# A fused two-block transformer kernel: the moving weights of the 512-column split products are read in another order

## The chip, the cores and the metric

The kernel runs on one core of one Trainium2 chip. The metric is the device time of one execution in microseconds. A core has TensorE (matrix products: it loads a 128 x 128 stationary operand and streams the columns of a moving operand past it), VectorE, ScalarE, GpSimd and a queue engine (SP) from which most DMAs are issued. Products write to PSUM, which VectorE and ScalarE read.

## The reference

One sequence of 256 tokens of width 2048 goes through two blocks in fp32. What matters here are the large projections and what is done with them:

```python
x = x + mix @ w_out[i]                                            # 2048 x 2048
h2 = rms_norm(x, mlp_norm[i])
x = x + jnp.square(jax.nn.relu(h2 @ w_ffn_up[i])) @ w_ffn_down[i]  # 2048 x 8192 x 2048
gate = jax.nn.sigmoid(rms_norm(x, ple_norm[i]) @ w_ple_gate[i])
x = x + gate * (p[i] @ w_ple_proj[i])
...
h = x + jnp.concatenate([gla_out, nsa_out], axis=-1) @ w_out
m = rms_norm_2(h, ffn_norm_g)
return h + (jax.nn.silu(m @ w_gate) * (m @ w_up)) @ w_down         # 2048 x 5632 x 2048
```

Between them stand the mixers (a causal pool, a chunked recurrence, gated linear attention, compressed and windowed attention).

## The kernel before, in words

Every engine has one program, written out by hand, and the programs meet at semaphores. Weights come through a ring of two slots in SBUF, each 16 tiles of 128 x 512, in groups numbered `n`. A slot has four units of 2,048 elements per partition. Each large product is a split one: the fp32 operand is held as a rounded part (`wh`, type fp32r) and the rest (`wl`), and `three` (L621) issues three fp32r products, high x high, high x low and low x high, into one sum in PSUM. ScalarE makes the high part of a unit (`high`, L1366), VectorE subtracts it to get the low part (`low`, L1899), in place in the ring; TensorE waits for `w_low`, uses the unit and reports `w_used`, upon which the next weights are loaded.

There are two kinds of split product. In `split_rows` (L628) the weights are stationary and 256 tokens move: FFN up projections, gates and inputs. In `split_tokens` (L665), and in two loops written like it for the second output projection (`first_half`, L1222, and the loop at L1307), the tokens are stationary and 512 columns of weights move: the output projections, the down projections of both FFNs and the PLE gate. The sums of these lie in two PSUM banks, one per half of the tokens (`pair[0]` and `pair[1]` in turn, `first_sums` in the attention stage), 512 neighbouring columns each. All products of both kinds are issued from L625.

VectorE adds the finished sums to the residual `xs` in chunks of 512 columns (`add_out`, L1901, and `add_first`, L2459), and in the PLE gate ScalarE takes them through a sigmoid into `gate_sb` (L1620). A pair of banks is written again after the addition of the call before last (`sum_step`). In the gate stage plain fp32 products with 512 columns (`project`, L1005, issued at L1012) stand among the split ones.

Of the kernel before, what the change touches and what calls it, by code (L numbers as in the profile page):

```python
# [14 lines left out]
ALU = mybir.AluOpType  # L15
ACT = mybir.ActivationFunctionType
# [6 lines left out]
KT = D // P  # L23
# [98 lines left out]
def build(nc, inp, consts, out):  # L122
# [26 lines left out]
    xs = sbuf("xs", [P, TT, D])  # L149
    actT = sbuf("actT", [P, KT, T], (0, KT * T))  # L150
# [47 lines left out]
    def along(ap, n):  # L198

        return ap.unsqueeze(len(ap.shape)).broadcast_to(list(ap.shape) + [n])  # L200

    ident, tri, eye64 = con("ident"), con("tri"), con("eye64")
    pair = [PS[:, 0:2, :], PS[:, 2:4, :]]
# [110 lines left out]
    rs_fin, rs_n4, rs_sq, rs_gate, rs_n5, scaled_ss = (small[:, 88 + 2 * i:90 + 2 * i] for i in range(6))  # L314
# [61 lines left out]
    gate_sb = split(actf[:, 3072:4096], (TT, CW))  # L376
# [34 lines left out]
    first_sums = [PS[:, 4:6, :], PS[:, 6:8, :], PS[:, 4:6, :], PS[:, 4:6, :]]  # L411

    XD, HD = area(XH_AT + 16, KT, T), area(0, KT, T)
    XH2 = HD
# [188 lines left out]
    def _(pe):  # L603
# [17 lines left out]
        def three(dst, weights, tokens, first, last, early=False):  # L621

            (wh, wl), (xh, xl) = weights, tokens
            for q, (w, x) in enumerate(((wh, xh), (wh, xl), (wl, xh))):
                mm = pe.matmul(dst, r32(w, early), r32(x, early), start=first and q == 0, stop=last and q == 2)  # L625
            return mm
# [38 lines left out]
        def split_tokens(n, out, xh, xl, i=None, per=2, units=UNITS[4], ready=None, after=None):  # L665

            for q, j in enumerate(units):
                pe.wait_ge(S["w_low"], split_count(n, j, i, per))
                if ready is not None:
                    ready(q)  # L670
                wh, wl = (a.rearrange("p (k n) -> p k n", k=4) for a in (high_home(n, i, j), unit_at(n % 2, j)))
                for k in range(4):
                    for t in range(TT):
                        x, tok = 4 * q + k, slice(t * P, (t + 1) * P)
                        mm = three(out[:, t, :], (xh(x)[:, tok], xl(x)[:, tok]), (wh[:, k, :], wl[:, k, :]),
                                   x == 0, x == 4 * len(units) - 1)
                mm.then_inc(S["w_used"], counts(units, j))
                if after and q in after:
                    after[q]()
# [42 lines left out]
        for t in range(2):  # L722
            mm = pe.transpose(PS[:, 5, t * P:(t + 1) * P], prow[:, t, :], ident)
# [46 lines left out]
        for g in range(2 * (NCH - 1)):  # L770
            c, m0 = g // 2, g % 2 * 4
            if g >= 4:
                pe.wait_ge(S["bk_copied"], g - 3)
            for m in range(4):
                mm = pe.transpose(PS[:, 4 + g % 4, m * P:(m + 1) * P], BK[:, m0 + m, c, :], ident)
# [123 lines left out]
        for c in range(NCH):  # L899
# [4 lines left out]
            for m in range(HM):  # L904
                for e in range(2):
                    mm = pe.matmul(PS[HALF[e], 0, m * C:(m + 1) * C], G[:, m, e, c, 0:C], UV(c)[:, m, e, :],
                                   start=True, stop=True)
# [7 lines left out]
            for m in range(HM):  # L915
                for e in range(2):
                    mm = pe.matmul(PS[HALF[e], 1, m * C:(m + 1) * C], DTi[HALF[e], m, c, :], ZSB[HALF[e], m, :],
                                   start=True, stop=True)
# [5 lines left out]
            if c < NCH - 1:  # L924
                for m in range(HM):
                    for e in range(2):
                        mm = pe.matmul(PS[HALF[e], 2, m * C:(m + 1) * C], BKtok(c)[:, m, e * C:(e + 1) * C],
                                       UV(c)[:, m, e, :], start=True, stop=True)
# [34 lines left out]
        for t in range(TT):  # L963
            pe.wait_ge(S["gate_copied"], t + 1)
            pe.wait_ge(S["yn_ready"], t + 1)
            for m in range(HM):
                mm = pe.transpose(PS[:, 4 + 2 * t + m // 4, m % 4 * P:(m % 4 + 1) * P], Ytok[:, t, m * P:(m + 1) * P], ident)
# [82 lines left out]
        for n in range(N_KCVC, N_GOQ):  # L1050
# [3 lines left out]
            if n == N_KSVS:  # L1054
                pe.wait_ge(S["w_low"], NARROW)
                for k in range(KT):
                    mm = three(PS[0:SWM, 4, 0:T], (SWH[:, k, :], SW[:, k, :]), (XH[:, k, :], actT[:, k, :]),
                               k == 0, k == KT - 1)
# [3 lines left out]
        for h in range(GH):  # L1062
            mm = pe.matmul(PS[:, 6 + h // 2, h % 2 * T:(h % 2 + 1) * T], GW2[:, h * P:(h + 1) * P], LR, start=True, stop=True)
        mm.then_inc(S["low_rank"], 1)
        for t in range(TT):
            mm = pe.transpose(PS[:, 5, t * 24:t * 24 + 24], LRG[32:SWM, t * P:(t + 1) * P], ident[32:SWM, 32:SWM])
# [77 lines left out]
        for i in range(2):  # L1144
            mm = pe.matmul(PS[:, 4 + i, :], con("ones"), KSQ[:, 2 * i:2 * i + 2, :].rearrange("p a b -> p (a b)"),
                           start=True, stop=True)
        mm.then_inc(S["k_sums"], 1)
        pe.wait_ge(S["nsq_ready"], 2)
        for t in range(TT):
            for h in range(NH):  # L1150
                mm = pe.matmul(PS[:, 6, t * NH + h:t * NH + h + 1], QSQ[:, h, t * P:(t + 1) * P], con("ones")[:, 0:1],
                               start=True, stop=True)
# [5 lines left out]
        for t in range(TT):  # L1158
            for h in range(GH):
                mm = pe.transpose(PS[:, 6 + t, h * P:(h + 1) * P], K4[:, h, t * P:(t + 1) * P], ident)  # L1160
# [16 lines left out]
        for i in range(2):  # L1177
            mm = pe.transpose(PS[:, 2, i * CB:(i + 1) * CB], PTAB[i], ident[0:CB, 0:CB])
# [35 lines left out]
        for t in range(TT):  # L1214
            pe.wait_ge(S["on_ready"], t + 1)
            for m in range(8):
                at = m % 2 * T + t * P
                mm = pe.transpose(PS[:, 4 + m // 2, at:at + P], OT[:, t, m * P:(m + 1) * P], ident)
# [3 lines left out]
        def first_half(*qs):  # L1222

            for q in qs:
                n, j, e, c = N_OUT2 + q // 8, q % 8 // 2, q % 2, q // 4
                if q % 4 == 0 and c >= 2:
                    pe.wait_ge(S["sum_step"], SUM["first2"] + 2 * c - 3)
                pe.wait_ge(S["w_low"], half_count(n, q % 8))
                if q < 4:
                    pe.wait_ge(S["gla_low"], q + 1)  # L1230
                if q == 0:
                    pe.wait_ge(S["on_read"], 4)
                wh, wl = (a.rearrange("p (k n) -> p k n", k=2) for a in (HIO[q % 4], half_at(n % 2, q % 8)))
                for k in range(2):
                    for t in range(TT):
                        x, tok = 2 * (q % 4) + k, slice(t * P, (t + 1) * P)
                        mm = three(first_sums[c][:, t, :], (XH2[:, x, tok], actT[:, x, tok]), (wh[:, k, :], wl[:, k, :]),
                                   x == 0, x == 7)
                mm.then_inc(S["w_used" if e else "half_used"], 1)

        first_half(0)
# [65 lines left out]
        for c in range(4):  # L1307
            n = N_REST2 + c // 2
            if c >= 2:
                pe.wait_ge(S["sum_step"], SUM["out2"] + c - 1)  # L1310
            for j in (2 * (c % 2), 2 * (c % 2) + 1):
                pe.wait_ge(S["w_low"], split_count(n, j))
                wh, wl = (a.rearrange("p (k n) -> p k n", k=4) for a in (high_home(n, i, j), unit_at(n % 2, j)))
                for k in range(4):
                    for t in range(TT):
                        x, tok = 8 + j % 2 * 4 + k, slice(t * P, (t + 1) * P)
                        mm = three(pair[c % 2][:, t, :], (XH2[:, x, tok], actT[:, x, tok]), (wh[:, k, :], wl[:, k, :]),
                                   x == 8, x == KT - 1)
                mm.then_inc(S["w_used"], 1)
                if j % 2 == 0 and c:  # L1320
                    turn("n5", c - 1)
# [34 lines left out]
    def _(act):  # L1356
# [59 lines left out]
        for j in range(1, KT // 2, 2):  # L1416
            act.wait_ge(S["norm_turned"], j + 1)
            for q in range(2):
                k = 2 * j + q
# [79 lines left out]
        for g in range(2 * (NCH - 1)):  # L1499
            c, m0 = g // 2, g % 2 * 4  # L1500
# [52 lines left out]
        for c in range(NCH):  # L1553
# [13 lines left out]
            if c % 2:  # L1567
                t = c // 2
# [38 lines left out]
        for c in range(4):  # L1607
            n = N_GATE + c
            high(n, (3,))
            if c == 0:  # L1610
                norm_chunk("n3", "ple_norm", 3)
                root("n3")
            else:
                norm_chunk("n4", None, c - 1)
            high(n + 1, (0, 1, 2))
            act.wait_ge(S["w_used"], used(n))
            act.wait_ge(S["rs_ready"], 2)
            act.wait_ge(S["sum_step"], SUM["gate"] + c)
            for t in range(TT):
                ins = act.activation(gate_sb[:, t], pair[c % 2][:, t], ACT.Sigmoid, scale=rs_gate[:, t:t + 1])  # L1620
            ins.then_inc(S["groups_read"], 1)
        def high_half(n, *qs):

# [222 lines left out]
    def _(v):  # L1846
# [54 lines left out]
        def add_out(w, g, at, by=None):  # L1901


            v.wait_ge(S["w_used"], w)
            if by is None:
                ins = v.tensor_tensor(xs[:, :, at], pair[g], xs[:, :, at], ALU.add)
            else:
                for t in range(TT):
                    ins = v.scalar_tensor_tensor(xs[:, t, at], pair[g][:, t], by[:, t:t + 1], xs[:, t, at], ALU.mult, ALU.add)  # L1909
            ins.then_inc(S["sum_step"], 1)  # L1910

        def columns(c):
            return slice(CW * c, CW * (c + 1))
# [545 lines left out]
        def add_first(c):  # L2459
            v.wait_ge(S["w_used"], 4 * N_OUT2 + 2 * c + 2)  # L2460
            for t in range(TT):
                r = xs[:, t, columns(c)]
                ins = v.scalar_tensor_tensor(r, r, rs_fin[:, t:t + 1], first_sums[c][:, t], ALU.mult, ALU.add)
            ins.then_inc(S["sum_step"], 1)

        def o_norm(t):
# [297 lines left out]
```

## Time and profile before

| | |
|---|---|
| median of 3 runs | 2439.66 us (2433.91 to 2442.28) |
| the profiled execution | 2437.74 us, span 2435.6 us |
| TensorE products busy | 2395.8 us, 98% of the span, 18,076 of them |
| weight loads busy | 2194.3 us, 90% |
| VectorE, ScalarE, GpSimd busy | 1358.3, 987.4, 191.5 us |
| HBM read | 420.75 MB, 174 GB/s over the span |

A group's row of the profile names the line, the engine, the operation, what it writes and reads, the shape and the count, then the busy time and the mean duration of one. Durations of products overlap, so the distance between the starts of two is read from the timeline.

### The profile page before, as it was taken

The numbers are of one execution on the slowest core, as the hardware profiler recorded it, in microseconds if no ns is written. First come the engines' busy times: TensorE is split into PE (matmuls) and PEld (weight loads), VectorE is DVE, ScalarE is ACT, GpSimd is POOL, SyncE is SP. The second block draws the span as 40 slices with busy tenths as digits, with TensorE's granted clock in tenths as the row PEclk, the third lists the DMA queues.
The fourth block names the chain that finished last, engine by engine and source line by source line (L and its number), as shares of the span: only waits on it lengthen the run. The fifth ranks groups of instructions, "written<-read, shape, count | busy, mean of one in ns | idle before, by whom it ended". The sixth has DMA issues, their size and how long they took to land.

```text
span 2435.6 us, 39206 instructions
## 1 busy us (share of the span) xinstructions
PE 2395.8 (98%) x18076; PEld 2194.3 (90%) x18076; DVE 1358.3 (56%) x1134; ACT 987.4 (41%) x932; POOL 191.5 (8%) x139
## 2 busy tenths in 40 slices
PE   8998999999999999999999999999999999999999
PEld 7997888998998998988789999877998999999897
DVE  5597665544454444455457568575554554555553
ACT  4652244443333333344453364265433333433332
POOL 0003110020110110210000002000000000000000
PEclk9999999999999999999999999999999999999999
DMA  7553146665656656664556544244554754755644
GB/s 219 167 161 88 31 174 217 185 202 182 202 188 195 198 184 202 181 239 173 190 150 201 178 141 140 89 152 140 173 191 163 234 192 163 229 181 178 214 158 138
DMA packets 334528, 425.36 MB, mean 175 GB/s; under 512 B 4185, under 2 KB 249357, under 8 KB 333981
## 3 DMA queue, kind: packets, MB, share of 16 engines
q1 hardware_dynamic: 333053, 418.55, 53.2%
q0 software_dynamic: 1136, 4.17, 0.6%
q8 instruction: 142, 2.33, 0.4%
q10 hardware_dynamic: 176, 0.14, 0.0%
q14 instruction: 21, 0.17, 0.0%
HBM read 420.75 MB, written 2.10 MB: 174 GB/s over the span
## 4 chain that ended last, share of the span: by engine, by line
PE 90%; DVE 5%; issue 2%; ACT 2%; DMA 0%; POOLq 0%; POOL 0%; DVEq 0%; ACTq 0%
PE PS L625 81%; PE PS L824 1%; PE PS L715 1%; DVE ring_r L1941 1%; PE PS L661 1%; PE PS L1012 1%; PE PS L1292 0%; DVE ring_r L2249 0%; PE PS L1196 0%; ACT arena_r L1366 0%; DVE arena L2052 0%; PE PS L896 0%; PE PS L951 0%; PE PS L1120 0%; PE PS L943 0%
## 5 line engine op out<-in xcount | busy, mean ns | idle before, releaser
L625 PE MATMUL PS<-arena_r,arena_r 128*128 128x256 f32 (+1 forms) x6944 | 1544.2, 300 | 3.7 <-DVE ring_r L2249 1.4
L625 PEld LDWEIGHTS PS<-arena_r,arena_r 128*128 128x128 f32 x6944 | 1123.5, 188 | 60.2 <-issue 4.3
L1899 DVE TENSOR_TENSOR ring_r<-ring,arena_r 128x2048 fp32r<-128x2048 f32 x316 | 730.5, 2315 | 658.7 <-ACT arena_r L1366 658.7
L1366 ACT ACTIVATE arena_r<-ring 128x2048 fp32r<-128x2048 f32 (+1 forms) x394 | 691.6, 1761 | 977.0 <-PE PS L625 971.4
L625 PE MATMUL PS<-arena_r,ring_r 128*128 128x256 f32 x3072 | 852.3, 277 | 0.0
L625 PEld LDWEIGHTS PS<-arena_r,ring_r 128*128 128x128 f32 x3072 | 578.5, 188 | 0.0
L625 PE MATMUL PS<-ring_r,arena_r 128*128 128x512 f32 (+1 forms) x1504 | 539.0, 371 | 0.0
L625 PE MATMUL PS<-arena_r,actT_r 128*128 128x512 f32 (+1 forms) x1184 | 454.3, 384 | 0.0
L625 PEld LDWEIGHTS PS<-ring_r,arena_r 128*128 128x128 f32 x1504 | 275.8, 188 | 49.7 <-issue 1.4
L625 PEld LDWEIGHTS PS<-arena_r,actT_r 128*128 128x128 f32 x1184 | 222.3, 188 | 44.6
L625 PE MATMUL PS<-actT_r,arena_r 128*128 128x256 f32 (+1 forms) x656 | 184.5, 281 | 0.0
L625 PE MATMUL PS<-ring_r,actT_r 128*128 128x256 f32 x832 | 156.5, 290 | 6.6 <-DVE ring_r L1941 6.6
L625 PE MATMUL PS<-ring_r,ring_r 128*128 128x256 f32 x512 | 146.0, 285 | 0.0
L625 PEld LDWEIGHTS PS<-ring_r,actT_r 128*128 128x128 f32 x832 | 132.3, 196 | 9.3 <-DVE ring_r L1941 7.2
L625 PEld LDWEIGHTS PS<-actT_r,arena_r 128*128 128x128 f32 (+1 forms) x656 | 123.8, 189 | 0.0
L2249 DVE TENSOR_TENSOR ring_r<-ring,arena_r 128x1024 fp32r<-128x1024 f32 x56 | 72.6, 1313 | 60.0 <-ACT arena_r L1366 59.9
L625 PEld LDWEIGHTS PS<-ring_r,ring_r 128*128 128x128 f32 x512 | 99.3, 194 | 0.0
L1941 DVE TENSOR_TENSOR ring_r<-ring,actT_r 128x2048 fp32r<-128x2048 f32 x26 | 59.5, 2292 | 40.4 <-ACT actT_r L1366 40.2
L2692 POOL TENSOR_TENSOR arena_r<-arena 128x1024 fp32r<-128x1024 f32 x16 | 30.3, 1895 | 612.6 <-ACT arena L1605 612.6
L2733 POOL TENSOR_TENSOR arena_r<-arena,cst 128x1024 fp32r<-128x1024 f32 x9 | 23.0, 2552 | 690.0 <-DVE arena L2637 690.0
L1909 DVE SCALAR_TENSOR_TENSOR xs<-PS,small,xs 128x512 f32<-128x512 f32 x64 | 45.1, 747 | 40.1 <-PE PS L625 40.1
L1366 ACT ACTIVATE actT_r<-ring 128x2048 fp32r<-128x2048 f32 x26 | 49.8, 1920 | 42.9 <-PE PS L625 42.9
(339 smaller groups left out, 1403.6 us busy)
## 6 DMA issues: line engine op xcount, KB each, us to landing
ring<-in_w_ffn_up SPq DMA_DIRECT2D x32, 2048.0 KB, 10.3
ring<-in_w_ffn_down SPq DMA_DIRECT2D x32, 2048.0 KB, 8.1
ring<-in_w_in SPq DMA_DIRECT2D x22, 2048.0 KB, 8.3
ring<-in_w_gate SPq DMA_DIRECT2D x22, 2048.0 KB, 8.1
ring<-in_w_up SPq DMA_DIRECT2D x22, 2048.0 KB, 8.1
ring<-in_w_in SPq DMA_DIRECT2D x32, 1024.0 KB, 5.3
ring<-in_w_out SPq DMA_DIRECT2D x16, 2048.0 KB, 8.2
ring<-in_w_down SPq DMA_DIRECT2D x12, 2048.0 KB, 8.1
```

What stands on the lines that cost most here:

```text
L625: mm = pe.matmul(dst, r32(w, early), r32(x, early), start=first and q == 0, stop=last and q == 2)
L661: mm = pe.transpose(PS[:, 8 - banks + j % banks, q * T + t * P:q * T + (t + 1) * P], xs[:, t, k * P:(k + 1) * P], ident)
L715: mm = pe.matmul(half(0)[0:n, f, :], wag[:, k, f * P:f * P + n], actT[:, k, :], start=(k == 0), stop=(k == KT - 1))
L824: mm = pe.matmul(PS[h, bank, at:at + C], lhs(h, m, c, e), rhs(h, m, c, e), start=True, stop=True)
L1012: mm = pe.matmul(PS[:, 4 + t, :], pT[:, k, t * P:(t + 1) * P], pproj[:, c, k, :], start=(k == 0), stop=(k == 1))
L1366: return act.activation(dst, src, ACT.Copy, scale=scale)
L1899: v.tensor_tensor(r32(u), u, high_of(high_home(n, i, j)), ALU.subtract).then_inc(S["w_low"], counts(units, j))
L1909: ins = v.scalar_tensor_tensor(xs[:, t, at], pair[g][:, t], by[:, t:t + 1], xs[:, t, at], ALU.mult, ALU.add)
L1941: v.tensor_tensor(r32(w), w, high_of(high_at(u), True), ALU.subtract).then_inc(S["in_low"], 1)
L2249: v.tensor_tensor(r32(u), u, high_of(HIH[q % 4]), ALU.subtract).then_inc(S["w_low"], 1)
L2692: pool.tensor_tensor(r32(XD[:, 4 * c:4 * c + 4]), r, r, ALU.mult)
L2733: pool.tensor_tensor(r32(HD[:, 4 * m:4 * m + 4]), RQ[1], one, ALU.mult).then_inc(S["ffn2_high"], 1)
```

## The change

The moving weights of all products with 512 columns are read through a view: where columns 0, 1, 2, ... 511 went in that order, now 0, 128, 256, 384, 1, 129, 257, 385, ... go. So the sum of column 128 h + i lies at place 4 i + h of its PSUM bank, and all readers of these sums take them with a step of four, and write the residual or the gate in the old order. The stationary operands, the number of products, of columns and of elements, and all waits stay as they are.

```diff
+    def woven(ap):
+        return ap.rearrange("p (h i) -> p i h", h=4)
+    def unwoven(ap):
+        return ap.rearrange("p (i h) -> p h i", h=4)
+    def halves_of(ap):
+        return ap.rearrange("p (h i) -> p h i", h=4)
...
@@ split_tokens; first_half and the loop after the attention alike
-                        mm = three(out[:, t, :], (xh(x)[:, tok], xl(x)[:, tok]), (wh[:, k, :], wl[:, k, :]),
-                                   x == 0, x == 4 * len(units) - 1)
+                        mm = three(out[:, t, :], (xh(x)[:, tok], xl(x)[:, tok]),
+                                   (woven(wh[:, k, :]), woven(wl[:, k, :])), x == 0, x == 4 * len(units) - 1)
...
@@ the sigmoid of the gate, ScalarE
-                ins = act.activation(gate_sb[:, t], pair[c % 2][:, t], ACT.Sigmoid, scale=rs_gate[:, t:t + 1])
+                ins = act.activation(halves_of(gate_sb[:, t]), unwoven(pair[c % 2][:, t]), ACT.Sigmoid, scale=rs_gate[:, t:t + 1])
...
@@ add_out, VectorE; add_first alike
             if by is None:
-                ins = v.tensor_tensor(xs[:, :, at], pair[g], xs[:, :, at], ALU.add)
+                r = xs[:, :, at].rearrange("p t (h i) -> p t h i", h=4)
+                ins = v.tensor_tensor(r, pair[g].rearrange("p t (i h) -> p t h i", h=4), r, ALU.add)
             else:
                 for t in range(TT):
-                    ins = v.scalar_tensor_tensor(xs[:, t, at], pair[g][:, t], by[:, t:t + 1], xs[:, t, at], ALU.mult, ALU.add)
+                    r = halves_of(xs[:, t, at])
+                    ins = v.scalar_tensor_tensor(r, unwoven(pair[g][:, t]), by[:, t:t + 1], r, ALU.mult, ALU.add)
```

## Rows read from the trace of the kernel before

**Rows 1.** The page's parts 1 and 2: busy time, busy tenths, granted clock.
```profile
PE 2395.8 (98%) x18076; PEld 2194.3 (90%) x18076; DVE 1358.3 (56%) x1134; ACT 987.4 (41%) x932; POOL 191.5 (8%) x139
...
PEclk9999999999999999999999999999999999999999
```
**Rows 2.** The page's part 4: the chain that ended last.
```profile
PE 90%; DVE 5%; issue 2%; ACT 2%; DMA 0%; POOLq 0%; POOL 0%; DVEq 0%; ACTq 0%
PE PS L625 81%; PE PS L824 1%; PE PS L715 1%; DVE ring_r L1941 1%; PE PS L661 1%; PE PS L1012 1%; PE PS L1292 0%; DVE ring_r L2249 0%; PE PS L1196 0%; ACT arena_r L1366 0%; DVE arena L2052 0%; PE PS L896 0%; PE PS L951 0%; PE PS L1120 0%; PE PS L943 0%
```
**Rows 3.** Groups of TensorE products by form: count, busy us, mean ns, idle before.
```profile
L625 PE MATMUL PS<-arena_r,arena_r 128*128 128x512 f32 x1344 | 508.8, 393 | 1.6 <-DVE actT_r L2626 1.2 <-DVE actT_r L2541 0.5
L625 PE MATMUL PS<-ring_r,arena_r 128*128 128x512 f32 x1248 | 486.7, 390 | 0.0
L625 PE MATMUL PS<-arena_r,actT_r 128*128 128x512 f32 x1120 | 436.2, 389 | 0.0
...
L625 PE MATMUL PS<-arena_r 128*128 128x512 f32 x32 | 13.1, 408 | 0.0
```
**Rows 4.** Timeline of TensorE, a down projection's beginning and end: start, us, what.
```profile
704.58 0.39 PE L625 MATMUL PS<-arena_r,arena_r 128*128 128x256 f32 x2
...
704.92 0.39 PE L625 MATMUL PS<-arena_r,arena_r 128*128 128x512 f32 x1
...
791.97 0.39 PE L625 MATMUL PS<-arena_r,arena_r 128*128 128x256 f32 x2
```
**Rows 5.** The instructions of L625 within 704.92 to 791.96: min/median/max ns.
```profile
L625 PE MATMUL PS<-arena_r,arena_r x129: 276/389/393, 704.7 to 791.3; 128*128 128x512 f32 x128, 128*128 128x256 f32 x1
```
**Rows 6.** Timeline of the gate stage: first split product, and what follows 72.
```profile
1185.70 0.79 PE L625 MATMUL PS<-arena_r,arena_r 128*128 128x512 f32 x1
...
1202.74 0.82 PE L661 MATMUL PS<-cst,xs 128*128 128x128 f32 x6
```
**Rows 7.** Windows over down projections: busy us of PE, PEld, DVE, ACT, POOL, clock, DMA.
```profile
530.60:617.60 87.00, 87.00 (x386) 72.05 (x385) 42.05 (x23) 31.59 (x17) 5.80 (x2) 1.00 0.60 193
...
704.92:791.96 87.04, 87.04 (x386) 72.09 (x385) 42.04 (x23) 31.59 (x17) 5.80 (x2) 1.00 0.60 193
1841.05:1906.35 65.30, 65.30 (x291) 54.08 (x290) 34.09 (x20) 21.09 (x11) 3.87 (x1) 1.00 0.59 199
```
**Rows 8.** What TensorE waited for: us in total, times, longest.
```profile
PE PS L685 <- DMA arena<-in_attn_norm: 8.5, 1, 8.5
```
**Rows 9.** Timeline of weight loads around the plain fp32 products of L1012.
```profile
1167.70 0.19 PEld L1012 LDWEIGHTS PS<-arena 128*128 128x128 f32 x1 [0.24 <-issue]
...
1170.71 0.19 PEld L625 LDWEIGHTS PS<-ring_r,arena_r 128*128 128x128 f32 x1 [0.24 <-issue]
```
**Rows 10.** GpSimd's groups with 240 elements: step of 64 bytes, and neighbours.
```profile
L2725 POOL COPY arena<-arena 128x240 f32<-128x240 f32 x8 | 9.3, 1211 | 21.9 <-PE PS L1102 21.9
...
L2681 POOL TENSOR_SCALAR xs<-xs 128x240 f32<-128x240 f32 x8 | 6.5, 810 | 0.1
```
**Rows 11.** VectorE's level products, L2325: min/median/max ns.
```profile
L2325 DVE TENSOR_TENSOR arena<-arena x6: 684/684/685, 1443.0 to 1479.4; 128x512 f32<-128x512 f32 x6
```
**Rows 12.** The page's part 5: the subtraction that makes the low parts.
```profile
L1899 DVE TENSOR_TENSOR ring_r<-ring,arena_r 128x2048 fp32r<-128x2048 f32 x316 | 730.5, 2315 | 658.7 <-ACT arena_r L1366 658.7
```
**Rows 13.** The readers of the sums, by line: min/median/max ns.
```profile
L1909 DVE SCALAR_TENSOR_TENSOR xs<-PS,small,xs x64: 741/744/753, 552.6 to 2431.7; 128x512 f32<-128x512 f32 x64
...
L1906 DVE TENSOR_TENSOR xs<-PS,xs x8: 1217/1221/1226, 374.9 to 1709.0; 128x1024 f32<-128x1024 f32 x8
...
L1620 ACT ACTIVATE actT<-PS,small x8: 667/679/687, 1167.5 to 1252.8; 128x512 f32<-128x512 f32 x8
```
**Rows 14.** The chain's last pieces.
```profile
2424.83 6.13 PE PS L625 x27
...
2430.99 0.75 DVE xs L1909
2431.74 0.66 DVEq L2738
```

More of the change, by code:

```diff
@@ L1236, in first_half @@
                         x, tok = 2 * (q % 4) + k, slice(t * P, (t + 1) * P)
-                        mm = three(first_sums[c][:, t, :], (XH2[:, x, tok], actT[:, x, tok]), (wh[:, k, :], wl[:, k, :]),
-                                   x == 0, x == 7)
+                        mm = three(first_sums[c][:, t, :], (XH2[:, x, tok], actT[:, x, tok]),
+                                   (woven(wh[:, k, :]), woven(wl[:, k, :])), x == 0, x == 7)
                 mm.then_inc(S["w_used" if e else "half_used"], 1)
@@ L1316, in _ @@
                         x, tok = 8 + j % 2 * 4 + k, slice(t * P, (t + 1) * P)
-                        mm = three(pair[c % 2][:, t, :], (XH2[:, x, tok], actT[:, x, tok]), (wh[:, k, :], wl[:, k, :]),
-                                   x == 8, x == KT - 1)
+                        mm = three(pair[c % 2][:, t, :], (XH2[:, x, tok], actT[:, x, tok]),
+                                   (woven(wh[:, k, :]), woven(wl[:, k, :])), x == 8, x == KT - 1)
                 mm.then_inc(S["w_used"], 1)
@@ L2461, in add_first @@
             for t in range(TT):
-                r = xs[:, t, columns(c)]
-                ins = v.scalar_tensor_tensor(r, r, rs_fin[:, t:t + 1], first_sums[c][:, t], ALU.mult, ALU.add)
+                r = halves_of(xs[:, t, columns(c)])
+                ins = v.scalar_tensor_tensor(r, r, rs_fin[:, t:t + 1], unwoven(first_sums[c][:, t]), ALU.mult, ALU.add)
             ins.then_inc(S["sum_step"], 1)
```

## The prediction

> **What bounds the kernel now.** I read the page first. TensorE's matmul row is busy for 98% of the span, the weight loads for 90%, VectorE for 56%, ScalarE for 41%, and the granted clock stands in the top tenth in all 40 slices [rows 1]. The chain that ended last is 90% TensorE, 81% of it on L625, the one line from which all split products are issued [rows 2]. The groups by form say what that line holds: 3,744 products with 512 moving columns (the four forms of [rows 3] whose shape ends in 512, 1,344 + 1,248 + 1,120 + 32) and a larger number with 256. Counting the loops that the diff edits gives the same number: 16 calls x 96 in the first FFN, 4 x 96 in the first output projection, 4 x 96 in the gate, 12 x 72 and 4 x 48 in the second FFN, 16 half units x 12 and 8 units x 24 in the second output projection, which is 3,744. So every 512-column product is touched and no 256-column one.
>
> A duration in a group's row (389 ns) is not what a product costs, since products overlap. The cost is the distance from one start to the next. I took it from the timeline where nothing else is in the way: the down projection of the first FFN's second part begins at 704.92 and ends where the next 256-column product begins, at 791.97 [rows 4], and the query of the line in that stretch counts 128 products with 512 columns in the form of its first row [rows 5]; two further forms take turns with it, so there are 384: 87.05 / 384 = 226.7 ns. The windows show the same for the first FFN's first part (87.00 us) and for the first part of the second FFN, 288 products in 65.30 us, 226.7 ns each [rows 7]; I count three such groups of each, 3 x 384 + 3 x 288 = 2,016 products. In the gate stage 72 products take from 1185.70 to 1202.74 [rows 6], 236.7 ns each, and nobody waits there either. I put the other 1,728 products at the middle of the two, 231.7, which makes a mean of (2,016 x 226.7 + 1,728 x 231.7) / 3,744 = 229 ns, 857 us in all, a third of the span.
>
> The other engines have room in such a stretch: with 87.04 us of TensorE go 42.04 of VectorE, 31.59 of ScalarE, and a DMA share of 0.60 [rows 7]. TensorE is idle for 2435.6 - 2395.8 = 40 us of the whole run [rows 1], and its longest wait for others is 8.5 us, at the start [rows 8]. So the time of this kernel is the number of products times their distance, and the question is what the new order of reading does to that distance.
>
> **The change, part by part.**
>
> *The order in which the moving weights are read.* Nothing is added or removed: the same 3,744 products, the same 512 columns, the same weight loads. Only the address steps: now each column is 4 bytes behind the one before; after the change each is 128 elements (512 bytes) on, and every fourth one comes back to the line next to where it was. No row of this trace has a TensorE operand read like that. I bound it from both sides.
>
> The nearest row on the same engine is the plain fp32 projection in the gate stage, which reads the same 4-byte elements. Its products start 0.43 us apart: from 1167.70 to 1170.71 are seven steps, 430 ns for 512 columns, 0.84 ns a column [rows 9]. This is one column for each period of the lower level of 1.2 GHz, while the granted clock is at 2.4 GHz, so it is the data type's pace. Half of it, one column a period of 2.4 GHz, would be 215 ns. The split products ask for one 4-byte column in 0.42 ns and get one in 0.443 (226.7 / 512): 6% short, and 10% short in the gate stage, where the operands lie in other places and nothing else differs. Both say that these products already run at the limit of the path that brings their operands from SBUF, and that this path minds addresses. A path that is short by 6% when neighbours are read in turn has nothing in hand for a worse order. If each column then needs an access of its own and gets one per period of 1.2 GHz, a product takes the 430 ns of the plain one. Cost: 3,744 x (430 - 229) = +753 us.
>
> The other rows on strides are of other engines. GpSimd copies 240 elements that lie 64 bytes apart in 1,211 ns, and scales 240 neighbours in 810 [rows 10]: 1.5 times. On TensorE that factor would be 343 ns a product (1.5 x 229), 3,744 x 114 = +427 us. VectorE pays nothing for a small step: the level products go down to single elements two apart, and all six forms stay at 684 to 685 ns for 512 elements [rows 11]. But VectorE takes an element in no less than 1.1 ns (2,048 in 2,315 ns [rows 12]), less than half TensorE's demand, so its rows can't excuse TensorE. The lower end is a gain: if the lost 6% comes from reading neighbours in turn, the new order may give it back, down to 215 ns, 3,744 x (215 - 229) = -52 us. The upper end is the 430 ns with the same 6% on top, 453 ns, 3,744 x 224 = +839 us. Of 215, 229, 343, 430 and 453 I take 430, because it is a pace that this engine shows for this element size and because the two 4-byte reads in one period of 1.2 GHz that the present pace needs are what neighbours in one line can give and elements 512 bytes apart cannot.
>
> The Trainium skill ("Advanced Engine Details and Errata", SBUF Cachelines) states that SBUF has lines of 16 bytes, and that a reader needs at least two hits on a line to absorb the access latency. The new order hits each line once before it leaves it. No row here shows that on TensorE. By that rule the sum has the sign that I give it; it names no factor.
>
> *Taking the sums out of PSUM with a step of four.* The additions to the residual (64 of 744 ns on L1909, 8 of 1,221 on L1906, and 8 on L2463 like those of L1909) and the sigmoid (8 of 679 on L1620) read PSUM 16 bytes apart now [rows 13]. Their element counts stay. No row reads PSUM so; bounds are nothing (VectorE's step of two was free) and twice the streaming part, some 0.5 us for 512 elements. What hides it: sums alternate between two pairs of banks, and a pair is wanted again only a whole call later, 21.8 us (96 x 226.7), while VectorE is idle for half of the stretch [rows 7]. Without that cover it would be 64 x 0.5 = 32 us. Only the last two additions are in the open: the chain ends with 6.13 us of products, 0.75 of L1909 and the store [rows 14]. That is 0 to +1 us; I take 0.
>
> *What follows elsewhere.* With slower products ScalarE, VectorE and the DMAs only gain slack. In the attention stage, whose 192 products stand between other waits, longer fillers can cover at most a part of TensorE's 40 idle us; I take off 0.
>
> **The sum.** The profiled execution took 2437.7 us (span 2435.6), 2 us under the median of 2439.7. 2437.7 + 753 = 3190 us.
>
> **Rivals.**
>
> *The order gives the lost share back (faster).* For it: the 6% is lost only where columns are read at 0.44 ns, never in the plain rows, whose 430 is exactly two periods a column, so it is a matter of how the elements come, and the gate stage proves that addresses change it. Against it: nothing shows that jumping is better than walking. It would take the product to 215 ns: 2437.7 - 52 = 2386 us. It decides as soon as a product comes out under 226 ns. The Trainium skill ("TensorE: Matmul & The Clock Gate", Part 1) gives 512 columns a distance of 215.7 ns at the full clock; the trace disagrees, with 226.7. By its figure a cured product would make an estimate of 2388 us.
>
> *Nothing happens to the distance (same).* If the 6% belongs to the array's handling of this data type, and the path has its own store of a few lines, four streams are as good as one: 2438 us. For it: 226.7 is very steady over 2,016 products. Against it: the 236.7 of the gate stage.
>
> *A partial penalty (slower, but less).* Each jump costs part of a period, as on GpSimd: 343 ns a product, 2437.7 + 427 = 2865 us.
>
> **How the numbers follow.** One column per period of 1.2 GHz, with or without the 6%: 0.40 (3190 to 3277, own range with slips 3100 to 3290). Partial penalty: 0.09. Worse than 3290, when more than one period is lost per jump: 0.05. No effect: 0.16. Share given back, whole or in part: 0.30. A measurement of this kernel tells a change from none at about 0.3%, 7 us. Slower 0.54, same 0.16, faster 0.30. The range must reach across, from 2380, below the whole gain, to 3290; it leaves out the worse case, and a gain beyond 57 us.
>
> **What would show it.** In the changed profile: starts of 512-column products 430 ns apart in the stretch of the first FFN (now 226.7), where one group of 384 then takes 165 us instead of 87; the 256-column products unchanged at some 113 ns (from 704.58 to 704.92 there are three [rows 4]); the mean duration of the 512 forms up by about 200 ns; idle time of ScalarE before L1366 and of VectorE before L1899 longer, since they wait for TensorE; L1909 at 744 ns would make the step of four free, 1.2 us would make it double. The forecast is wrong if the starts are 215 to 229 ns apart. It is wrong in size if they are neither near 229 nor near 430.

## The result, and the profile after

The changed kernel takes 2619.21 us (median of 4 runs, 2613.64 to 2620.76) against 2440.97 us before: a ratio of 1.0731, with a 95% interval of 1.0704 to 1.0759. It is slower, by 178 us, where 3190 us, 753 more, were forecast. The time lies within the stated range, but that range was wide enough to hold three cases.

The page of the changed kernel, its parts 1 and 2 (they answer to [rows 1]):
```profile
PE 2579.0 (99%) x18076; PEld 2203.8 (84%) x18076; DVE 1359.1 (52%) x1134; ACT 987.7 (38%) x932; POOL 191.7 (7%) x139
...
PEclk9999999999999999999999999999999999999999
```
TensorE is busy for 183 us more, nearly the whole difference of the spans (2617.3 - 2435.6 = 181.7 us). VectorE, ScalarE and the clock have not moved. The groups of TensorE products by form (count, busy us, mean ns) say which products these are; those with 512 columns answer to [rows 3]:
```profile
L637 PE MATMUL PS<-arena_r,arena_r 128*128 128x256 f32 x5568 | 1030.1, 277 | 2.1 <-DVE ring_r L2263 1.4 <-DVE actT_r L1902 0.7
L637 PE MATMUL PS<-arena_r,ring_r 128*128 128x256 f32 x3072 | 851.8, 277 | 0.0
L637 PE MATMUL PS<-arena_r,arena_r 128*128 128x512 f32 x1344 | 577.6, 445 | 0.5 <-DVE actT_r L2555 0.5
L637 PE MATMUL PS<-ring_r,arena_r 128*128 128x512 f32 x1248 | 551.0, 442 | 0.0
L637 PE MATMUL PS<-arena_r,actT_r 128*128 128x512 f32 x1120 | 494.0, 441 | 0.0
```
The 256-column products stay at 277 ns; the 512-column ones go from 389 to 393 up to 441 to 445. The timeline of the same down projection as in [rows 4] (start, us, what) gives their distance:
```profile
742.10 0.43 PE L637 MATMUL PS<-arena_r,arena_r 128*128 128x512 f32 x1
742.37 0.44 PE L637 MATMUL PS<-ring_r,arena_r 128*128 128x512 f32 x1
...
847.05 0.40 PE L637 MATMUL PS<-arena_r,arena_r 128*128 128x256 f32 x2
```
(847.05 - 742.10) / 384 = 273.3 ns, where it was 226.7: 46.6 ns more. The window over it and the one over the first part of the second FFN (78.7 us for 288 products, 273.3 ns) answer to [rows 7]:
```profile
742.10:847.05 104.95, 104.95 (x386) 72.77 (x385) 42.12 (x23) 31.57 (x17) 5.80 (x2) 1.00 0.48 160
1972.92:2051.60 78.68, 78.68 (x291) 54.54 (x290) 34.09 (x20) 21.10 (x11) 3.87 (x1) 1.00 0.51 170
```
(The 288 products of that part run from 1972.76 to 2051.47.) TensorE has no idle time there, the clock is full, and VectorE and ScalarE do what they did before in a longer time. 2,016 products at 46.6 ns are 94 us; the other 1,728 are left with 88 us, 51 ns each. The gate stage bears this out: its 72 products, which took 236.7 ns each [rows 6], take (1307.10 - 1286.39) / 72 = 287.6 ns:
```profile
1286.39 0.84 PE L637 MATMUL PS<-arena_r,arena_r 128*128 128x512 f32 x1
...
1307.10 0.49 PE L673 MATMUL PS<-cst,xs 128*128 128x128 f32 x3
```
Added up over all split products with 512 columns but the last, the time from each start to the start of the next product is 859.7 us before and 1041.5 us after: 181.8 us, the whole difference of the spans. The readers of the sums, by line (min/median/max ns), answer to [rows 13]:
```profile
L1923 DVE SCALAR_TENSOR_TENSOR xs<-PS,small,xs x64: 739/744/752, 576.2 to 2613.3; 128x512 f32<-128x512 f32 x64
```
```profile
L1919 DVE TENSOR_TENSOR xs<-PS,xs x8: 1217/1224/1226, 378.8 to 1840.8; 128x1024 f32<-128x1024 f32 x8
```
```profile
L1632 ACT ACTIVATE actT<-PS,small x8: 671/682/688, 1265.8 to 1365.7; 128x512 f32<-128x512 f32 x8
```
The step of four in PSUM is free on both engines: 744 ns as before, 1,224 for 1,221, 682 for 679. What grew elsewhere is ScalarE's wait for TensorE (971.4 us before) and behind it VectorE's wait for ScalarE (658.7 us before); the columns are us in total, times, longest:
```profile
ACT arena_r L1378 <- PE PS L637: 1127.2, 298, 10.1
DVE ring_r L1911 <- ACT arena_r L1378: 772.4, 272, 8.0
```
So all of the cost is in the order in which TensorE reads its moving columns. Why 273, and not 430 or 227, is what the experiments ask.

### The profile page after: what moved, and what is told of

It is laid out like the page before. It is cut to its first block, busy times and chain, and to the rows that moved or that the text cites. A ratio compares the mean times of both kernels' runs of the same rounds, so it can differ in the third digit from the quotient of the medians.

```text
span 2617.3 us, 39206 instructions
## 1 busy us (share of the span) xinstructions
PE 2579.0 (99%) x18076; PEld 2203.8 (84%) x18076; DVE 1359.1 (52%) x1134; ACT 987.7 (38%) x932; POOL 191.7 (7%) x139
## 4 chain that ended last, share of the span: by engine, by line
PE 92%; DVE 5%; ACT 2%; issue 1%; DMA 0%; DVEq 0%; ACTq 0%
PE PS L637 84%; PE PS L836 1%; PE PS L727 1%; DVE ring_r L1955 1%; PE PS L1024 1%; PE PS L673 1%; DVE ring_r L2263 0%; PE PS L1208 0%; PE PS L1304 0%; ACT arena_r L1378 0%; DVE arena L2066 0%; PE PS L908 0%; PE PS L963 0%; PE PS L1132 0%; PE PS L955 0%
## 5 line engine op out<-in xcount | busy, mean ns | idle before, releaser
L637 PE MATMUL PS<-arena_r,arena_r 128*128 128x256 f32 (+1 forms) x6944 | 1612.7, 310 | 2.6 <-DVE ring_r L2263 1.4
L637 PE MATMUL PS<-ring_r,arena_r 128*128 128x512 f32 (+1 forms) x1504 | 603.2, 414 | 0.0
L637 PE MATMUL PS<-arena_r,actT_r 128*128 128x512 f32 (+1 forms) x1184 | 512.1, 432 | 0.0
```

## The experiments

On TensorE all of them (but e10) change only the order of the 512 moving columns. The readers follow. e1, e2, e8, e9 and e10 put the columns back in the old order; e3 to e7 and e11 to e15 leave that out and take the sums as they lie, so that columns of the output are exchanged. In all of them the 8 additions of L1919 are made as 16 of 512 columns. "Distance" is always taken as above, over the 384 products of the first FFN's second down projection; TensorE is busy throughout that stretch in every run. Times of a single execution stand beside the kernel before on the same chip: 2432.57 us for e1 to e4, 2437.11 for e5 to e8, 2436.55 (median of 9) for e11 and e12, 2435.54 for e13 to e15.

### Which property of the order costs: e1 to e4

```diff
     def woven(ap):
-        return ap.rearrange("p (h i) -> p i h", h=4)            # 0 128 256 384 1 ...   the changed kernel
+        return ap.rearrange("p (h i) -> p i h", h=2)            # e1: 0 256 1 257 2 ...
+        return ap.rearrange("p (i h) -> p h i", h=4)            # e2: 0 4 8 ... 508 1 5 ...
+        return ap.rearrange("p (q l e) -> p l q e", q=4, e=4)   # e3: 0-3 128-131 256-259 384-387 4-7 ...
+        return ap.rearrange("p (l a b) -> p l b a", a=2, b=2)   # e4: 0 2 1 3 4 6 5 7 ...
```
e1. 

> The moving columns come from two halves of 256 in turn instead of four quarters (0, 256, 1, 257, ...); the readers of the sums take a step of two. The changed kernel has 273.3 ns between the starts of two products in the down projections, against 226.7 before. Theory A (lines): a column costs extra when it is not on the 16-byte line of the column before it, whatever the pattern; then 512 jumps here as there, 273 ns and about 2617 us. Theory B (wraps of the pattern): what costs is each end of the inner loop of the access pattern, 46.6 ns for 128 ends, 0.36 ns each; here there are 256 ends, 320 ns a product, about 2438 + 3744 x 0.0932 = 2790 us. Theory C (distance): the reader minds how far apart the streams lie or how many there are; with two streams 1024 bytes apart anything from 227 to 273 ns.

e2. 

> The columns are read in four passes with a step of four elements (0, 4, 8, ..., 508, 1, 5, ...): every column lies on the next 16-byte line, and the pattern's inner loop ends only 4 times a product. Theory A (lines): 512 jumps to another line, 273 ns, about 2617 us. Theory B (wraps): 4 ends cost 1.5 ns, 228 ns, about 2443 us. Theory C (distance, streams): neighbouring lines are no distance, 227 ns, about 2440 us. If each new line costs a whole period of 1.2 GHz, as the prediction had it: 430 ns, 3190 us.

e3. 

> Four neighbouring columns (one line of 16 bytes) are read from each quarter in turn: 0 to 3, 128 to 131, 256 to 259, 384 to 387, 4 to 7, ... The readers of the sums take them in the order in which they lie, so that the columns of each chunk of 512 are exchanged in the output. A new line comes every four columns, as in the kernel before, but 512 bytes away, and the inner loop of four ends 128 times, as in the changed kernel. Theory A (lines): 128 lines, 227 ns, about 2440 us. Theory B (wraps): 128 ends, 273 ns, about 2617 us (more if the second loop's 32 ends cost extra). Theory C (distance): between, since a quarter is left every fourth column.

e4. 

> The four columns of each 16-byte line are read in the order 0, 2, 1, 3, and the lines in their old order; the readers take the sums as they lie, so that columns 1 and 2 of every four are exchanged in the output. No jump to another line beyond those of the kernel before, but the inner loop of two ends 256 times. Theory A (lines): 227 ns, about 2440 us. Theory B (wraps): 256 ends, 320 ns, about 2790 us. Theory C (distance): 227 ns, 2440 us.

Measured: e1 2397.34 us, e2 3309.3, e3 2589.24, e4 2443.43. Timeline of e1, beginning and end of the down projection:
```profile
695.20 0.38 PE L637 MATMUL PS<-arena_r,arena_r 128*128 128x512 f32 x1
695.42 0.38 PE L637 MATMUL PS<-ring_r,arena_r 128*128 128x512 f32 x1
...
778.08 0.40 PE L637 MATMUL PS<-arena_r,arena_r 128*128 128x256 f32 x2
```
82.88 / 384 = 215.8 ns: two halves in turn are not only free, they give back 10.9 of the 13.4 ns that one stream loses against 512 columns at 2.4 GHz (213.3 ns). The same of e2:
```profile
885.65 0.62 PE L637 MATMUL PS<-arena_r,arena_r 128*128 128x512 f32 x1
...
1062.78 0.42 PE L637 MATMUL PS<-arena_r,arena_r 128*128 128x256 f32 x2
```
177.13 / 384 = 461.3 ns, near the 430 to 453 ns that the prediction had put on the changed kernel. In e2 the readers take neighbours from PSUM and step by four elements in SBUF; they take longer for it, in the shadow of TensorE (ScalarE 1,172 ns for 682, and on VectorE):
```profile
L1924 DVE SCALAR_TENSOR_TENSOR xs<-PS,small,xs x64: 1109/1186/1222, 665.7 to 3303.2; 128x512 f32<-128x512 f32 x64
```
The timelines of e3 and e4:
```profile
736.43 0.43 PE L637 MATMUL PS<-arena_r,arena_r 128*128 128x512 f32 x1
...
839.33 0.41 PE L637 MATMUL PS<-arena_r,arena_r 128*128 128x256 f32 x2
```
```profile
706.00 0.39 PE L637 MATMUL PS<-arena_r,arena_r 128*128 128x512 f32 x1
...
793.06 0.39 PE L637 MATMUL PS<-arena_r,arena_r 128*128 128x256 f32 x2
```
268.0 and 226.7 ns. Theory A (every change of line costs the same) falls with e1 (216 instead of 273) and with e2 (461 instead of 273). Theory B (ends of the inner loop) falls with e1 and e4, where 256 ends cost nothing, and with e2, where 4 ends go with the dearest order. Theory C is left in some form: places, or streams.

### How far apart, or how many: e5 to e8

```diff
+        return ap.rearrange("p (a b i) -> p i b a", a=2, b=2)   # e5: 0 256 128 384 1 ...
+        return ap.rearrange("p (g h i) -> p g i h", g=2, h=2)   # e6: 0 128 1 129 ..., then 256 384 ...
+        return ap.rearrange("p (g h i) -> p g i h", g=16, h=2)  # e7: 0 16 1 17 ... 15 31, 32 48 ...
+        return ap.rearrange("p (h i) -> p i h", h=8)            # e8: 0 64 128 ... 448 1 65 ...
```
e5. 

> The same four quarters as in the changed kernel, but in the order 0, 2, 1, 3 (columns 0, 256, 128, 384, 1, ...); the readers take the sums as they lie, so the columns of each chunk are exchanged in the output. So far: one stream 226.7 ns between starts in the down projections, two halves 1024 bytes apart 215.8, four quarters 273.3. Theory D (places): what counts is the address bits in which neighbours in time differ; reads one after the other want to differ in the bit of 1024 bytes, and in the order 0, 1, 2, 3 every second step does not. Reordered, every step changes that bit: 216 ns, about 2397 us. Theory E (streams): what counts is how many lines are open at a time, four being too many in any order: 273 ns, about 2617 us.

e6. 

> Two streams as in the version with halves, but 512 bytes apart instead of 1024: first columns 0 to 255 (0, 128, 1, 129, ...), then 256 to 511. The readers take the sums as they lie, so columns are exchanged in the output. Theory D (places): if 512 bytes is the bad distance, 227 to 273 ns or more, 2440 to 2617 us or more. Theory E (streams): two are two, 216 ns, about 2397 us.

e7. 

> Two streams 64 bytes apart: in each 32 columns the two runs of 16 in turn (0, 16, 1, 17, ...). The readers take the sums as they lie. Theory D (places): another distance, another time; by the 6% that one stream loses (32 array periods in 512 columns, one for each 64 bytes), 64 bytes apart may be as bad or as good as 1024; no number follows, only that it differs from 216. Theory E (streams): 216 ns, about 2397 us.

e8. 

> Eight runs of 64 columns in turn (256 bytes apart), the readers take a step of eight. Theory E (streams): more than four lines open, 273 ns or up to the 461 ns of the step of four, where no line is read twice in a row: 2617 to 3310 us. Theory D (places): steps of 256 bytes, the bit of 1024 changes in one step of four, worse than the changed kernel's one in two: over 273 ns. A reader that keeps a line for some columns makes 273; one that has room for four lines makes 461.

Measured: e5 2616.19 us, e6 2399.56, e7 2399.29, e8 3401.69. Timelines of e5, e6 and e7:
```profile
742.37 0.43 PE L637 MATMUL PS<-arena_r,arena_r 128*128 128x512 f32 x1
...
847.32 0.40 PE L637 MATMUL PS<-arena_r,arena_r 128*128 128x256 f32 x2
```
```profile
697.56 0.38 PE L637 MATMUL PS<-arena_r,arena_r 128*128 128x512 f32 x1
...
780.44 0.40 PE L637 MATMUL PS<-arena_r,arena_r 128*128 128x256 f32 x2
```
```profile
697.28 0.38 PE L637 MATMUL PS<-arena_r,arena_r 128*128 128x512 f32 x1
...
780.16 0.40 PE L637 MATMUL PS<-arena_r,arena_r 128*128 128x256 f32 x2
```
273.3 ns for the four quarters in the other order, and 215.8 for two streams at 512 bytes (e6) and at 64 (e7). So the distance between two streams has no effect from 64 to 1024 bytes, and theory D (places) falls. The number has. Eight in turn, e8:
```profile
901.99 0.71 PE L637 MATMUL PS<-arena_r,arena_r 128*128 128x512 f32 x1
...
1088.93 0.42 PE L637 MATMUL PS<-arena_r,arena_r 128*128 128x256 f32 x2
```
186.94 / 384 = 486.8 ns. This is above the 461 ns that theory E had as its most; only theory D, which e5 to e7 rule out, had left room for it.

### Blocks of 64 bytes: e11 and e12

```diff
+        return ap.rearrange("p (g q i) -> p g i q", g=32, q=4)  # e11: 0 4 8 12 1 5 9 13 ..., then 16 20 ...
+        return ap.rearrange("p (g q i) -> p g i q", g=16, q=8)  # e12: 0 4 8 ... 28 1 5 ..., then 32 36 ...
```
e11. 

> Four streams again, but only 16 bytes apart: in each 64 bytes the four lines in turn (columns 0, 4, 8, 12, 1, 5, ...), then the next 64 bytes. The readers take the sums as they lie. Theory E (lines): four lines of 16 bytes open at a time, as in the changed kernel: 273 ns, about 2617 us. Theory F (blocks): the reader fetches and keeps blocks of 64 bytes, one stream loses one array period for each block (32 in 512 columns, just the 6%), two blocks in turn hide it, four don't fit; here one block at a time is in use: 227 ns, about 2440 us.

e12. 

> Eight streams 16 bytes apart: in each 128 bytes the eight lines in turn. The readers take the sums as they lie. Theory E (lines): eight lines open, 487 ns as with eight eighths, about 3400 us. Theory F (blocks): two blocks of 64 bytes, of each four columns in turn: 216 to 227 ns, about 2400 to 2440 us.

Measured: 2587.93 and 3376.28 us, with 268.3 and 480.0 ns. Timeline of e11, then of e12:
```profile
734.90 0.43 PE L637 MATMUL PS<-arena_r,arena_r 128*128 128x512 f32 x1
...
837.94 0.40 PE L637 MATMUL PS<-arena_r,arena_r 128*128 128x256 f32 x2
```
```profile
896.90 0.64 PE L637 MATMUL PS<-arena_r,arena_r 128*128 128x512 f32 x1
...
1081.20 0.43 PE L637 MATMUL PS<-arena_r,arena_r 128*128 128x256 f32 x2
```
Four and eight lines that lie side by side cost within 2% of what four and eight far ones do. Theory F (blocks of 64 bytes are kept) falls. A unit of 16 bytes fits these runs; no run tests it against a smaller one.

### Jumps without return, and visits of two columns: e13 to e15

```diff
+        return ap.rearrange("p (h i e) -> p i h e", h=2, e=4)   # e13: 0-3 256-259 4-7 ...
+        return ap.rearrange("p (l s e) -> p s l e", s=2, e=4)   # e14: 0-3 8-11 16-19 ..., then 4-7 12-15 ...
+        return ap.rearrange("p (h i e) -> p i h e", h=4, e=2)   # e15: 0 1 128 129 256 257 384 385 2 3 ...
```
e13. 

> Whole lines from two halves in turn: columns 0 to 3, 256 to 259, 4 to 7, 260 to 263, ... The readers take the sums as they lie. If each jump to a line that is not the next one costs (e3: 268 ns with 128 such jumps, one array period of 0.42 ns each over 215), 268 ns here too, about 2590 us. If what costs is that more than two places are read in turn, 216 ns as with halves column by column (2397 us), or 227 ns as with one stream if the gain needs a change of line at every column (2440 us).

e14. 

> One stream that reads whole lines, first every even line, then every odd one (columns 0 to 3, 8 to 11, 16 to 19, ...): 128 jumps over one line, none back but one. The readers take the sums as they lie. If a jump to a line other than the next costs an array period: 268 ns, about 2590 us. If only the number of places in turn counts: 227 ns, about 2440 us.

e15. 

> Four quarters in turn as in the changed kernel, but two columns at each visit (0, 1, 128, 129, 256, 257, 384, 385, 2, 3, ...). The readers take the sums as they lie. If the number of lines in turn counts, 268 to 273 ns as with one column (e, the changed kernel) and with four (e3) at a visit: about 2590 to 2617 us. If changes of line are what costs, there are half as many as in the changed kernel: about 245 ns, 2510 us.

Measured: 2525.48, 2458.48 and 3248.45 us. Timelines of e13, e14 and e15:
```profile
724.28 0.42 PE L637 MATMUL PS<-arena_r,arena_r 128*128 128x512 f32 x1
...
820.32 0.40 PE L637 MATMUL PS<-arena_r,arena_r 128*128 128x256 f32 x2
```
```profile
709.99 0.39 PE L637 MATMUL PS<-arena_r,arena_r 128*128 128x512 f32 x1
...
799.58 0.40 PE L637 MATMUL PS<-arena_r,arena_r 128*128 128x256 f32 x2
```
```profile
872.68 0.65 PE L637 MATMUL PS<-arena_r,arena_r 128*128 128x512 f32 x1
...
1042.93 0.44 PE L637 MATMUL PS<-arena_r,arena_r 128*128 128x256 f32 x2
```
250.1, 233.3 and 443.4 ns. None of the stated readings holds. e13 is not 216, 227 or 268, so jumps to a line that isn't the next cost something, but not one fixed price. e15 was expected at 245 to 273 and takes 443: four lines in turn, as in the changed kernel, with half the changes of line, and it is far dearer. So "how many lines are in turn" is not the rule either. Nor is it the number of visits: e15 makes 256 of two columns, e2 512 of one, and they take 0.87 and 0.90 ns a column. What sets e15 apart is that a line's second pair of columns comes seven columns after its first, where in the changed kernel a line is taken up again after four.

### The best order, timed, and the 256-column products: e9 and e10

e9 is e1 again. e10 adds, for the up projections and the second FFN's gate:
```diff
-                                   (xh[:, k0 + k, :], xl[:, k0 + k, :]), k0 + k == 0, k0 + k == KT - 1)
+                                   (turned(xh[:, k0 + k, :]), turned(xl[:, k0 + k, :])), k0 + k == 0, k0 + k == KT - 1)
...
+                    if p in ("n2", "n5"):    # tokens_high; tokens_low alike: in memory, even tokens first
+                        dst, src = halves_of(dst), unwoven(src)
+                    ins = copy(dst, src, by)
```
Here `turned` is the order of e1 for 256 columns.

e9. 

> The version with two halves again, timed in five rounds against the kernel before: 215.8 ns instead of 226.7 between starts in the down projections, 3,744 products; its one look gave 2397 us. Both standing theories (streams; blocks) expect 0.983 of the time before, some 40 us less.

e10. 

> As the version with two halves, and the 256 moving columns of the FFN up projections and the second FFN's gate (7,296 products, some 113 to 120 ns now) are read as two halves of 128 in turn too. Their tokens are stored so that the sums come out in the old order: the copies and subtractions that write them take the transposed tokens out of PSUM with a step of two. If one stream loses 6% at any length, 256 columns go from 113.3 to 109 ns (256 columns at 2.4 GHz and the 2.5 ns that 512 columns now keep): 7,296 x 4 to 8 ns = 30 to 60 us less than with the halves alone, 2340 to 2370 us. If the weight loads (188 ns each, overlapped, busy for 87.3 of 87.3 us in these stretches) are what holds the 256-column products, nothing: 2397 us.

Measured against the kernel before (2436.55 us, median of 9): e9 2397.65 us (median of 4), ratio 0.9837 (0.9821 to 0.9854); e10 2381.58 us (median of 5), ratio 0.9769 (0.9751 to 0.9787). So e9 is 1.6% faster than the kernel before and e10 2.3%, both clear of the noise. In e10 the 768 products between the end of one down projection and the start of the next:
```profile
774.55 0.39 PE L637 MATMUL PS<-arena_r,arena_r 128*128 128x256 f32 x2
```
```profile
860.31 0.38 PE L637 MATMUL PS<-arena_r,arena_r 128*128 128x512 f32 x1
```
85.76 / 768 = 111.7 ns, where the kernel before has 87.3 / 768 = 113.7 (from 617.6 to 704.92). Over 7,296 products the 2 ns are 15 us, and 16 were measured between the two medians. Neither of the two stated outcomes came, 109 ns or no gain. What holds the last 2 to 3 ns was not tried; weight loads are under way for 85.75 of these 85.76 us, so the rival that the expectation names, the loads, stays open for that rest.

## Why the prediction was wrong, point by point

**The bound, the counts, the cover: right.** Only the 3,744 products with 512 columns changed; their distances add up to the whole difference (181.8 us); every other engine only waited more.

**The step that failed:** "If each column then needs an access of its own and gets one per period of 1.2 GHz, a product takes the 430 ns of the plain one." Its condition fails: a new line at each column does not by itself cost an access. The changed kernel takes each column from another line than the one before and needs 273 ns; e1 does the same and needs 215.8. The price was near the mark for other orders: e2, in which no line is taken up again before 128 columns have passed, costs 461 ns, 0.90 ns a column. That this is the price of one access for each column isn't shown either, since e15, where every second column lies in the line just read, takes 0.87 ns a column. What I had not weighed is that a line just read may still be at hand some columns later, which is a reading of the runs and not shown by one alone. One of the prediction's own rivals had the thought ("the path has its own store of a few lines"), but as a reason for no effect at all.

**The sum by its terms.** Forecast: 3,744 x 201 ns = +753 us. Measured: 46.6 ns in the clean groups, 48.5 on the mean (181.7 us / 3,744). The rival of a partial penalty (343 ns, from GpSimd's factor of 1.5) had the right sign but 114 ns for 48.5, and its mechanism, part of a period for each jump, fails with e1, which jumps at every column and loses nothing. It had 0.09 of the chance.

**The weighing of the ends.** I put weight on "a path that is short by 6% when neighbours are read in turn has nothing in hand for a worse order". e1 contradicts it: two halves in turn, each column in another line than the one before, run at 215.8 ns, 5% faster. So the right sign of the forecast is in part luck: it is owed to the four runs of this change, and the same argument would have called two runs slower too. Most of the 6% was a loss of reading in one stream, as the faster rival had it, and its floor of 215 ns was near; it just needs two streams and not four. The forecast price of that case, 2386 us, stands against 2397.65 for e9, a gain of 39 us (2436.55 - 2397.65) where 52 were priced. The Trainium skill ("TensorE: Matmul & The Clock Gate", Part 1) gives 215.7 ns for 512 columns; the trace before disagreed, the trace of e1 agrees.

**The gate stage was misread.** I took its 236.7 ns as proof that addresses matter, "and nothing else differs". Part of it was something else. The start of the first of the 72 products is on record 0.63 us before the second's (kernel before):
```profile
1185.70 0.79 PE L625 MATMUL PS<-arena_r,arena_r 128*128 128x512 f32 x1
1186.33 0.39 PE L625 MATMUL PS<-ring_r,arena_r 128*128 128x512 f32 x1
```
The weight loads show why. Each load starts with the product before it; the steps are 0.43 us up to 1186.10 and 0.23 us from there:
```profile
1185.67 0.19 PEld L625 LDWEIGHTS PS<-arena_r,arena_r 128*128 128x128 f32 x1 [0.24 <-issue]
1186.10 0.19 PEld L625 LDWEIGHTS PS<-ring_r,arena_r 128*128 128x128 f32 x1 [0.24 <-issue]
1186.33 0.19 PEld L625 LDWEIGHTS PS<-arena_r,arena_r 128*128 128x128 f32 x1
```
So 0.40 us of the 0.63 belong to the last plain fp32 product, which starts at 1185.67, and the split product pays no more than the others. Without it (1202.74 - 1186.33) / 71 = 231.1 ns, so 4.4 of the 10 ns are left. They run from 226 to 237 ns in an order that comes again every twelve products, and are gone in e1. That fits the places of the operands; no run moved them, so it stays argued.

**The step of four in PSUM: right.** It was taken at nothing, from a range of 0 to +1 us, and the durations did not move.

**What fits all runs, and what stays open.** Ordered by how many columns pass until a line is taken up again: after 2 columns 215.8 ns (e1, e6, e7), after 4 columns 268.3 to 273.3 (e11, e5, the change), after up to 7 columns 443.4 (e15), after 8 columns 480.0 to 486.8 (e12, e8), after 128 columns 461.3 (e2). Lines that are read whole and not taken up again: 226.7 when the next line follows, 233.3 with every second line, 250.1 from two halves, 268.0 from four quarters. That a line is kept for about four columns and not for seven is a reading of this list after the fact: no run was made to test it alone. The Trainium skill ("Advanced Engine Details and Errata", SBUF Cachelines) states that a reader needs at least two hits on a line of 16 bytes to absorb the access latency. e2, with one hit at a time and 461.3 ns, agrees. e1, with one hit at a time and 215.8 ns, and e15, with two hits at each visit and 443.4 ns, do not, so the measurements decide: hits in a row do not order these runs. Not settled are why one stream loses 6% against 213.3 ns and two lose 1%, why whole lines from two or four places cost 250 and 268, why the step of four is a little cheaper than eight in turn, and what three, five or six runs in turn would cost, which would test the reading.

## What to carry to other kernels

When a stream of products has no idle time, take the distance between starts and compare it with the columns at the granted clock: 226.7 ns where 512 columns at 2.4 GHz are 213 is a loss worth an experiment. Before a new order is put through a whole kernel, time it at two, four and eight ways and with a plain step: here two were 1.6% faster, four 7% slower, eight 40% slower, and the one known point did not tell their order. A loss at the present order does not say on which side of it the other orders lie.

## What the runs showed of the hardware that was not expected

- fp32r products with 512 moving columns: 226.7 ns apart with columns in one run, 215.8 with two runs in turn (64, 512 or 1024 bytes apart), 273.3 with four, 486.8 with eight, 461.3 with a step of four elements. The granted clock was 1.00 in the window over that down projection in every run.
- Exchanging the columns within each group of four (0, 2, 1, 3) changes nothing: 226.7 ns.
- VectorE and ScalarE read PSUM with a step of four fp32 elements at the pace of neighbours: 744 ns for 512 elements either way, and 682 against 679. With the same step in SBUF, where the result goes (and on VectorE one input too), and neighbours in PSUM, as e2 has it, they take 1,186 and 1,172 ns.
- With two runs in turn, the differences between stages go too: the gate stage's 72 products take 221.4 ns each in e1 (236.7 before), and without the first one, whose start is recorded while a plain fp32 product is still ahead of it, (1177.09 - 1161.76) / 71 = 215.9 ns.
- A product's recorded start can lie within the time of the product before it: behind plain fp32 ones it is 0.03 us after the last one's start and 0.40 us before that one's 0.43 us are over. The distance of a group is safer from its second product on.
